# Up projections of three feed-forwards as seven half products instead of eight, with block sums of the weights

## The reference, cut to what matters

```python
def swiglu(h, w_gate, w_up, w_down):
    return jnp.dot(jax.nn.silu(jnp.dot(h, w_gate)) * jnp.dot(h, w_up), w_down)

x = x + 0.5 * swiglu(rmsnorm_2(x, ffn1_norm[layer]), ffn1_w_gate[layer], ffn1_w_up[layer], ffn1_w_down[layer])
...                                            # mixer
x = x + 0.5 * swiglu(rmsnorm_2(x, ffn2_norm[layer]), ffn2_w_gate[layer], ffn2_w_up[layer], ffn2_w_down[layer])
```

## Time and profile before

| what | value |
|---|---|
| median of 3 runs | 3855.47 us (3851.02 to 3858.65) |
| span of the profiled execution | 3857.1 us |
| TensorE busy | 3750.6 us, 97% |
| VectorE, ScalarE, GpSimd busy | 1964.6, 1334.7, 390.9 us |
| the three stages' place | `s_up10` from about 1941 us, `s_up20` from about 2462, `s_up21` to the end |

### The profile page before, as it was taken

The page is one execution under the profiler, slowest core; times in us unless marked ns, Lnnn a source line. Parts: engine busy times, 40 slices in busy tenths (PEclk is TensorE's granted clock), DMA queues, the critical chain, the costliest instruction groups (busy, mean ns, idle before and its releaser), DMA issues.

```text
span 3857.1 us, 44920 instructions
## 1 busy us (share of the span) xinstructions
PE 3750.6 (97%) x18180; PEld 3048.8 (79%) x18180; DVE 1964.6 (51%) x3059; ACT 1334.7 (35%) x2194; POOL 390.9 (10%) x296
## 2 busy tenths in 40 slices
PE   7999999999999998999999999999999999979999
PEld 4868778888888866788888886888877888658888
DVE  5446566755546355544443457534453344574443
ACT  3245443323234334323332236322242222473222
POOL 0000002850000010000010011101020001101000
PEclk8899999999999989999999999999999999999999
DMA  5200012343322201233233332333222333203332
GB/s 214 91 28 1 1 50 81 131 134 120 121 92 76 61 28 34 87 98 98 93 99 93 98 99 82 92 97 96 93 88 88 99 98 93 67 19 97 96 97 93
DMA packets 105821, 329.99 MB, mean 86 GB/s; under 512 B 11536, under 2 KB 13200, under 8 KB 105616
## 3 DMA queue, kind: packets, MB, share of 16 engines
q1 hardware_dynamic: 103024, 320.38, 26.1%
q10 hardware_dynamic: 2592, 6.74, 0.5%
HBM read 324.99 MB, written 2.10 MB: 85 GB/s over the span
## 4 chain that ended last, share of the span: by engine, by line
PE 88%; DVE 3%; ACT 1%; issue 1%; POOL 0%; ACTq 0%; DVEq 0%
PE ps L673 23%; PE ps L674 23%; PE ps L675 23%; PE ps L1544 2%; PE ps L1529 1%; PE ps L1519 1%; PE ps L1520 1%; PE ps L1424 1%; PE ps L1426 1%; PE ps L1425 1%; PE ps L2637 1%; PE ps L2635 1%; PE ps L2601 1%; DVE t L3396 1%; PE ps L1516 0%
## 5 line engine op out<-in xcount | busy, mean ns | idle before, releaser
L673 PE MATMUL ps<-t 128*128 128x512 f32 (+1 forms) x4480 | 1689.0, 377 | 12.4 <-DVE t L297 9.0
L674 PE MATMUL ps<-t 128*128 128x512 f32 (+1 forms) x4480 | 1675.5, 374 | 0.0
L675 PE MATMUL ps<-t 128*128 128x512 f32 (+1 forms) x4480 | 1674.1, 374 | 0.0
L673 PEld LDWEIGHTS ps<-t 128*128 128x128 f32 x4480 | 848.9, 189 | 173.0 <-DVE t L297 10.8
L674 PEld LDWEIGHTS ps<-t 128*128 128x128 f32 x4480 | 848.9, 189 | 152.9 <-issue 5.9
L675 PEld LDWEIGHTS ps<-t 128*128 128x128 f32 x4480 | 848.3, 189 | 149.9
L297 DVE TENSOR_TENSOR t<-t 128x1024 fp32r<-128x1024 f32 (+1 forms) x517 | 645.9, 1249 | 442.4 <-ACT t L288 439.1
L288 ACT ACTIVATE t<-t 128x1024 fp32r<-128x1024 f32 (+1 forms) x517 | 533.2, 1031 | 780.0 <-PE ps L675 674.2
L1288 POOL TENSOR_TENSOR t<-t 128x512 f32<-128x512 f32 x88 | 113.8, 1293 | 1218.2 <-ACT t L1275 1218.2
L1318 DVE SCALAR_TENSOR_TENSOR t<-ps,t 128x512 f32<-128x512 f32 x96 | 66.4, 692 | 236.3 <-PE ps L675 236.3
L1278 ACT ACTIVATE t<-t 128x512 fp32r<-128x512 f32 x88 | 55.6, 632 | 340.3 <-DVE t L1308 340.3
(11 more groups left out here) (381 smaller groups left out, 3461.9 us busy)
## 6 DMA issues: line engine op xcount, KB each, us to landing
t<-w_s_up SPq DMA_DIRECT2D x176, 512.0 KB, 3.6
t<-w_up SPq DMA_DIRECT2D x88, 512.0 KB, 3.7
t<-w_ada SPq DMA_DIRECT2D x160, 256.0 KB, 3.0
t<-w_s_down SPq DMA_DIRECT2D x64, 512.0 KB, 3.6
t<-w_down SPq DMA_DIRECT2D x32, 512.0 KB, 3.7
t<-w_s_down SPq DMA_DIRECT2D x32, 384.0 KB, 3.0
t<-w_ada SPq DMA_DIRECT2D x16, 512.0 KB, 10.6
t<-w_rec_in SPq DMA_DIRECT2D x16, 512.0 KB, 3.7
```

What stands on the lines that cost most here:

```text
L673: k.T.matmul(out, wh, hh, start=(i == 0), stop=False)
L674: k.T.matmul(out, wh, hl, start=False, stop=False)
L675: ins = k.T.matmul(out, wl, hh, start=False, stop=(i == len(kts) - 1))
```

## The change

Three of the second block's four feed-forwards (`s_up10`, `s_up20`, `s_up21`; not `s_up11`) take their up products in units of two hidden tiles. A unit is a 2x2 block product: the weights' rows of blocks are gate and value, their columns are the even and the odd feature tiles, and the activations' blocks are feature parity by token half. In place of eight products of quarters, each unit makes seven (`PARTS`): three with a plain quarter of the weights (A11, A12, A22) and four with a sum of quarters: S1 = A21 + A22, S2 = S1 - A11, S3 = A22 - S2, S4 = A12 - S2. Each is 24 matmuls of 256 columns. The order is A11, S1, A12, S2, S3, S4, A22.

GpSimd makes the four sums in the raw slots (`Stream.sum`), 128x1024 each; every part, plain or summed, is then split by ScalarE and VectorE as a chunk was. The stages have three more raw slots and one more pair, and splits are issued three products ahead (`look`). Each quarter is loaded by two transfers of 256 KB, whose contiguous pieces are 128 elements long. In a unit A11, A21, A22, A12 are loaded in this order; the slot of A22 for the next unit comes free with the split of S3, that of A12 with the split of S4.

Three PSUM banks serve a unit: the products A11, S2, S3 and A22 go to the first, S1 and S4 to the second, A12 to the third. Partial sums are copied out between (`act_keep`) and added by VectorE (`dve_even`).

The activation's blocks and their differences T1 to T4 are made by `BlockFeed` in place of `Feed` in the stage before: ScalarE writes scaled feature tiles (`scaled`), GpSimd subtracts T1 (per pair p of feature tiles) and T2 to T4, of 128x256 each; ScalarE and VectorE write high and low parts in three pieces per pair: 512, 512 and 768 columns. In the last pair VectorE makes T2 to T4 itself, and GpSimd makes S1 and S2 of the first unit between T1 and its last two sums of squares. In the recurrent stage and the key stage some buffers are placed elsewhere. The diff's core:

```diff
+SEVEN = ("s_up10", "s_up20", "s_up21")
+PARTS = ("A11", "S1", "A12", "S2", "S3", "S4", "A22")
+QUARTERS = ("A11", "A12", "A21", "A22")
...
+    def look(self, c):
+        for a, b in ((self.begin[x], self.finish[x]) for x in SEVEN):
+            if c < a <= c + 2:
+                return a
+            if a <= c < b:
+                return max(min(c + 3, b - 1), c + 2)
+        return c + 2
...
+    def sum(self, name, u, part):
+        k, at = self.k, self.sums[name, u]
+        slot = {p: self.slot(x) for p, (n, x, t) in at.items()}
+        split = {p: self.lo_done.at(n + 1) for p, (n, x, t) in at.items()}
+        if part == "S1":
+            k.pool.wait_ge(at["S1"][2])
+            k.pool.wait_ge(at["A22"][2])
+            k.G.tensor_tensor(slot["S1"], slot["S1"], slot["A22"], ALU.add).then_inc(self.made.sem, 1)
+        elif part == "S2":
+            k.pool.wait_ge(self.made_at(name, u, "S1"))
+            k.pool.wait_ge(split["A11"])
+            k.G.tensor_tensor(slot["S2"], slot["S1"], slot["A11"], ALU.subtract).then_inc(self.made.sem, 1)
+        elif part == "S3":
+            k.pool.wait_ge(self.made_at(name, u, "S2"))
+            k.pool.wait_ge(split["S1"])
+            k.G.tensor_tensor(slot["S3"], slot["A22"], slot["S2"], ALU.subtract).then_inc(self.made.sem, 1)
+        else:
+            k.pool.wait_ge(self.made_at(name, u, "S2"))
+            k.pool.wait_ge(split["A12"])
+            k.G.tensor_tensor(slot["S4"], slot["A12"], slot["S2"], ALU.subtract).then_inc(self.made.sem, 1)
...
+class BlockFeed:
+    E, T1, O, T2, T3, T4 = (slice(256 * a, 256 * b) for a, b in ((0, 2), (2, 3), (3, 5), (5, 6), (6, 7), (7, 8)))
+    SPANS = (slice(0, 512), slice(512, 1024), slice(1024, 1792))
...
+    def act(self, m, free=()):
+        k, (p, odd) = self.k, divmod(m, 2)
+        for t in free:
+            k.act.wait_ge(t)
+        if m == 7:
+            k.stream.split_hi(self.first + 1)
+        k.act.wait_ge(self.finished(m, 0))
+        k.act.wait_ge(self.at("beside", 4 * p))
+        k.act.wait_ge(self.at("lo", 3 * p - 1 if odd else 3 * p - 2))
+        k.A.activation(self.Y[:, self.O if odd else self.E], k.X[:, m, :], ACT.Copy, scale=self.gain(m))\
+            .then_inc(self.sem["scaled"], 1)
+        if odd:
+            self.act_hi(p, 1)
+            if m == 7:
+                self.act_hi(p, 2)
+            self.act_square(m)
+        else:
+            if p:
+                self.act_hi(p - 1, 2)
+            self.act_square(m)
+            self.act_hi(p, 0)
...
+    def dve(self, m, free=()):
+        k, Y, (p, odd) = self.k, self.Y, divmod(m, 2)
+        for t in free:
+            k.dve.wait_ge(t)
+        if odd:
+            if m == 7:
+                k.stream.split_lo(self.first + 1)
+                k.dve.wait_ge(self.at("scaled", 8))
+                k.dve.wait_ge(self.at("beside", 13))
+                k.dve.wait_ge(self.at("lo", 9))
+                k.V.tensor_tensor(Y[:, self.T2], Y[:, 768:1024], Y[:, self.T1], ALU.subtract).then_inc(self.sem["late"], 1)
+                k.V.tensor_tensor(Y[:, self.T3], Y[:, 768:1024], Y[:, 0:256], ALU.subtract).then_inc(self.sem["late"], 1)
+                k.dve.wait_ge(self.at("late", 1))
+                k.V.tensor_tensor(Y[:, self.T4], Y[:, 1024:1280], Y[:, self.T2], ALU.subtract).then_inc(self.sem["late"], 1)
+            self.dve_lo(p, 1)
+            if m == 7:
+                self.dve_lo(p, 2)
+        else:
+            if p:
+                self.dve_lo(p - 1, 2)
+            self.dve_lo(p, 0)
...
+def seven_ffn(k, up, down, following=None):
+        blocks = (0, 1, 3, 4, 5, 2, 6)
...
+        def pe_unit(u, c):
+            for q in range(7):
+                w = st.operand(c + q, up, (u, PARTS[q]), 8)
+                if q == 0:
+                    x_bank[u], before = k.banks.take(ev.at(7 * u + 6))
+                elif q == 1:
+                    y_bank[u], before = k.banks.take(ev.at(7 * u + 4))
+                elif q == 2:
+                    z_bank[u], before = k.banks.take(ev.at(7 * u + 1))
+                elif q == 3:
+                    before = sn.at(3 * u + 1)
+                elif q == 4:
+                    before = sn.at(3 * u + 3)
+                elif q == 5:
+                    before = sn.at(3 * u + 2)
+                else:
+                    before = ev.at(7 * u + 3)
+                k.pe.wait_ge(before)
+                bank = (x_bank, y_bank, z_bank, x_bank, x_bank, y_bank, x_bank)[q][u]
+                for f in range(2):
+                    out = bank[:, 256 * f:256 * f + 256]
+                    for p in range(4):
+                        if u == 0:
+                            k.pe.wait_ge(source.ready(p, blocks[q]))
+                        bh, bl = (t[:, p, 256 * blocks[q]:256 * blocks[q] + 256] for t in (source.blocks.hi, source.blocks.lo))
+                        wh, wl = w.k(4 * f + p)
+                        k.T.matmul(out, wh, bh, start=(q < 3 and f == 0 and p == 0), stop=False, skip_group_check=True)
+                        k.T.matmul(out, wh, bl, start=False, stop=False, skip_group_check=True)
+                        ins = k.T.matmul(out, wl, bh, start=False, stop=(p == 3), skip_group_check=True)
+                ins.then_inc(pd.sem, 1)
+                st.used[c + q] = pd.at(7 * u + q + 1)
+                if u == 0 and q == 2:
+                    source.pe_sum()
...
+        def act_keep(u, q):
+            src, slot = {0: (x_bank, 1), 1: (y_bank, 2), 3: (x_bank, 0)}[q]
+            k.act.wait_ge(hl.at(u - 1))
+            k.act.wait_ge(pd.at(7 * u + q + 1))
+            k.A.activation(UT[:, u % 2, slot, :], src[u], ACT.Copy).then_inc(sn.sem, 1)
+        def act_silu(u, h):
+            a = UT[:, u % 2, h, :]
+            k.act.wait_ge(ev.at(7 * u + (2 if h else 5)))
+            k.A.activation(a, a, ACT.Silu).then_inc(si_.sem, 1)
+        def act_hidden(u):
+            k.act.wait_ge(dd.at(8 * ((2 * u - HID) // 8) + 8) if 2 * u >= HID else None)
+            k.act.wait_ge(ev.at(7 * u + 7))
+            k.A.activation(hidden(hid.hi, u), UT[:, u % 2, 0:2, :].rearrange("p h (f t) -> p h f t", f=2), ACT.Copy)\
+                .then_inc(hh.sem, 1)
...
+            left = None
+            for kind, g, j, c in steps:
+                if kind == "up":
+                    for q in range(7):
+                        st.split_hi(st.look(c + q))
+                        if q == 0 and left is not None:
+                            act_hidden(left)
+                        if q in (0, 1, 3):
+                            act_keep(j, q)
+                        if j == 0 and q == 3:
+                            source.act_root()
+                        if q == 4:
+                            act_silu(j, 1)
+                        if q == 6:
+                            act_silu(j, 0)
+                    left = j
...
+        def pool_scale(u, h):
+            slot = 1 if h else 2
+            a = halves(UT[:, u % 2, slot, :])
+            if h:
+                k.pool.wait_ge(si_.at(2 * u + 1))
+            else:
+                k.pool.wait_ge(ev.at(7 * u + 3))
+            k.pool.wait_ge(source.rstd())
+            k.G.tensor_tensor(a, a, factor(h), ALU.mult).then_inc(rm.sem, 1)
+        def pool_program():
+            last = {9 // 2: 0, 17 // 2: 0, 10: 0}
+            for u in range(n_units):
+                if u in (0, 5, 9):
+                    if u:
+                        st.sum(up, u, "S1")
+                        st.sum(up, u, "S2")
+                st.sum(up, u, "S3")
+                st.sum(up, u, "S4")
+                near = u not in (4, 8, 10)
+                if near:
+                    st.sum(up, u + 1, "S1")
+                pool_scale(u, 1)
+                if near:
+                    st.sum(up, u + 1, "S2")
+                pool_scale(u, 0)
...
+        def dve_even(u, q):
+            t2, t1, b2 = (UT[:, u % 2, x, :] for x in range(3))
+            k.dve.wait_ge(pd.at(7 * u + (3 if q == 3 else q + 1)))
+            if q == 3:
+                k.dve.wait_ge(sn.at(3 * u + 1))
+                k.V.tensor_tensor(t1, t1, z_bank[u], ALU.add).then_inc(ev.sem, 1)
+                k.dve.wait_ge(ev.at(7 * u + 1))
+                k.V.tensor_tensor(halves(t1), halves(t1), factor(1), ALU.mult).then_inc(ev.sem, 1)
+            elif q == 4:
+                k.dve.wait_ge(sn.at(3 * u + 2))
+                k.V.tensor_tensor(b2, b2, x_bank[u], ALU.add).then_inc(ev.sem, 1)
+            elif q == 5:
+                k.dve.wait_ge(sn.at(3 * u + 3))
+                k.V.tensor_tensor(t2, t2, y_bank[u], ALU.add).then_inc(ev.sem, 1)
+                k.dve.wait_ge(ev.at(7 * u + 4))
+                k.V.tensor_tensor(halves(t2), halves(t2), factor(0), ALU.mult).then_inc(ev.sem, 1)
+            else:
+                k.dve.wait_ge(rm.at(2 * u + 1))
+                k.V.tensor_tensor(t1, x_bank[u], t1, ALU.mult).then_inc(ev.sem, 1)
+                k.dve.wait_ge(rm.at(2 * u + 2))
```

(32 more changed lines are left out.)

377 lines of the change are left out of this document (329 added, 48 removed).

## The result

The changed kernel takes 3900.73 us (median of four runs, 3899.51 to 3907.06) where the kernel before, run beside it, takes 3855.45: 1.0123 times as long, 95% interval 1.0108 to 1.0137. The forecast was 3913, slower. The profiled execution spans 3898.2 us, 41.1 more than the 3857.1 of before.

The account below looks back on a forecast made before the run. TensorE, busy 97% of 3857.1 us, was taken to bound the kernel. The terms -55 + 30 + 45 + 34 + 4 = +58 on 3855.5 gave 3913 us, 1.5% slower; range 3850 to 3948.

Parts of the forecast that it names:

- the loop's term: Units' split-and-sum loop: a round of 23.4 us against TensorE's 21.0 makes the fourth product wait, +45 us.
- TensorE's work: Up products of three feed-forwards: seven half products of 2.87 us replace four of 5.44 in 33 units, -55 us.
- The copy: Before each unit's fifth product TensorE idles for ScalarE's whole copy of the fourth, 0.91 us in 33 units, +30 us.
- VectorE and GpSimd: Their mutual exclusion delays S2's split before the fourth product: 15 units per stage pay 2.5 us, +45 us.
- its round: Longest loop, from A22's load through GpSimd's sums and scalings to S3's split and low half: 23.4 us against 21.0.
- rival 1: Held VectorE or GpSimd instructions lose at most 0.56 us; loop costs 6, start 24: 3864 us, chance 0.15.
- The start: Start of the three stages: late blocks, splits and norm leave TensorE waiting 13, 10.5 and 10.5 us, +34 us.
- The ends: End of each stage: the third group's down products wait 1.3 us for the last hidden tiles, +4 us.
- Rival 2: VectorE's work fits GpSimd's waits, loop stays under 21.0, starts cost 3 us each: -12, 3843 us, chance 0.17.
- Rival 3: Small-piece weight transfers land after 7 us instead of 4, lengthening the loop by 3: +63, 3975 us, chance 0.05.
- Rival 4: The up products don't get shorter, because weight loads of 0.19 us set the pace; chance 0.03.

Follow-up runs that it names:

- The half copies: Changed kernel with a unit's first bank as two half-filled banks, so ScalarE copies one half while TensorE fills the other: 3893.97 us, ratio 1.0110.
- tiny sums: Changed kernel with GpSimd's weight sums on 32 of 1024 columns, all waits kept: 3838.64 us, ratio 0.9963.
- freeing the splits of A12 and S2: Half-copy kernel with norm-factor products reading PSUM; ScalarE also copies A12's and S2's high parts to PSUM, where VectorE subtracts them: 3847.24 us, ratio 0.9984.
- an operand in PSUM: Changed kernel with VectorE's splits in the three stages subtracting a zero tile in PSUM instead of the high part, sums whole: 3854.77 us, ratio 1.0005.
- freeing two products that TensorE did not wait for: Half-copy kernel with VectorE writing the two sums it multiplies by the norm factor into PSUM: 3883.78 us, ratio 1.0081.
- the kernel before with halved products: Kernel before with up products as 256-column matmuls, each with its own weight load: 3911.8 us with token halves inside, 3911.11 us with them outside.

## Why the prediction was right

The mechanism and four of the five terms held; one term was mis-sized, and inside the loop's term two errors cancelled. By its own steps:

**TensorE's work: forecast -55, measured -78.5.** This is the step that was off: the sum was 17 us too high by span (58 against 41), this term 23.5 too high and the four others together 6.5 too low. "Half the columns thus cost 2.87 and not 2.72" was read from one product of another stage. In the seven products it is 2.72 or 2.82. Of the 23.5 us, 231 x 0.05 = 11.6 come from the slow pace being 2.82 and not 2.87, and 117 x 0.10 = 11.7 from the half of the products that run at the fast one. The first units of the third groups take 20.5 us, copy included, the second ones, with 0.8 before the fourth product, 21.0 to 21.3 (forecast 21.0 for both).

**The copy: forecast +30, measured +34.2**, 0.94 before the fifth product and 0.08 behind its first matmul, where the weight load is not hidden. The forecast had 0.91, with 0.06 for that load, which none of its rows shows. The half copies showed that the wait itself can be removed whole, and that removing it gives 7 to 10 us and not 31.

**VectorE and GpSimd: forecast +45, measured +47.3.** The place is right (the fourth product, S2's split), and so is the cause, by the two experiments that make these waits vanish, one by taking the sums away and one by taking only the exclusion away. The working was less exact than its sum, and that the two agree is partly luck. It had 18 units paying 2.5; there are 23 (eight, seven and eight), paying 0.8 to 4.4 and 2.1 in the mean, and 7.2 us of it are not idle time but matmuls at the lower clock. (The terms of its round add up to 23.3 and not 23.4.) Splits that "stood still for all but 0.15 of the overlap" are there, now with 2.19 us of standing still where the longest row of before had 0.56, so rival 1 (no wait over 0.56) is refuted. Its 2.5 for a sum is near that of a sum alone, 2.4; in company the 132 sums have a mean of 2.92 (forecast over 2.9).

**The start: forecast +34, measured +33.4.** In the first stage the waits up to the third product are 4.2, 1.3 and 2.9, 8.4 against 8.3; the fourth and fifth product together pay 1.7 beyond the normal copy wait and the seventh 2.9 (forecast 1.8 and 2.8). The other two were put at 10.5 each and came out near 11.7 and 8.9. With tiny sums 24 us remain, the copy's 3 among them, so 20.8 against the 20 that the forecast gave without the exclusion; but that kernel shortens the sums as well, and so can't tell the two apart. Without the exclusion of the weight splits alone the starts did not shrink (39.1). So the exclusion that counts there would be another one, of the blocks' low parts and differences against the sums: in the kernel after the low parts of two blocks together last 3.93 us, beside sum S1.

```profile
1930.66 3.93 DVE L1173 TENSOR_TENSOR blocks_lo<-t,blocks_hi 128x768 fp32r<-128x768 f32 x2 [2.21 <-ACT blocks_hi L1146]
1930.99 3.05 POOL L436 TENSOR_TENSOR t<-t 128x1024 f32<-128x1024 f32 x1
```

That reading is from the trace; no kernel here took those instructions apart.

**The ends: forecast +4, measured +4.6** as the rest of the span; nothing tested it alone, and since that rest varies by up to 9 us from kernel to kernel, it bears out no more than that the term is small.

**The rivals.** Rival 2 (the loop hides, faster) did not come true, but it is near: "it decides from 2.4 us less in the round" fits what freeing the splits of A12 and S2 did, after which the fourth product waits no more. Rival 3 (late loads, landing after 7 us) is out by the page of the kernel after, transfers with their median time from issue to landing:

```profile
t<-w_s_up SPq DMA_DIRECT2D x144, 256.0 KB, 3.5
raw_more<-w_s_up SPq DMA_DIRECT2D x120, 256.0 KB, 4.1
```

The sum S1 does wait for its loads, 286 us of GpSimd's idle time in all, as the forecast's round has it. With an operand in PSUM it still does, 272 us, and the waits before the fourth product are gone. (For this rival 3913 + 63 is 3976, not 3975.) Rival 4 (no gain from half the columns) is out at 2.72 to 2.82.

**The lower clock: no term in the sum.** The five terms price every matmul at the full clock. Waits of under 3 us before the fourth product, such as the one of 2.37, were followed by 3 us at 0.50. It cost 7.2 us in the loop and some 4 at the starts, which the terms "before the fourth product" and "starts" took in without having foreseen it.

## What to carry to other kernels

When two engines exclude each other, price a change by the sum of what they do exclusively and look for the one instruction whose result is awaited: freeing two of the seven splits took the whole wait away, freeing two products that TensorE did not wait for left it at 52 us. A wait removed shows up in the terms next to it, in later waits and even in the pace of the engine, so compare all terms of the sum and not the one that was edited. A pace read in one stage is worth a bound from both sides before it is multiplied by 5544.

## What was not expected of the hardware

Matmuls of 256 columns, each with its own weight load, have two steady paces in the same code at a granted clock of 1.00, 0.1133 and 0.1178 us. They keep the one they are in for as long as nothing waits; of 128 changes in eleven kernels 127 stand at a wait. A wait of 0.73 us turned slow into fast 17 of 21 times; the waits before the fourth product, 0.3 to 3.2 us by start times, did so 6 of 42 times over all kernels. The same shapes in the kernel before with halved products ran at 0.1200, whatever the order of the loops, and there no wait stands between them. What sets the pace, why one wait changes it and another does not, and why those are 0.1200 and the seven products 0.1178, is open. In the kernel after, waits of over 2 us before the fourth product were followed by 3 us at half the clock five times of nine, which made the one of 2.4 cost 4.0.
